# Loading each expert weight unit with one transfer of 16 KB rows in place of two of 8 KB rows

## The chip, the cores and the metric

The kernel runs on one core of one Trainium2 chip. The metric is the device time of one execution in microseconds (us), median over several runs; lower is better. All arithmetic is in float32.

## What is computed

The reference is a small encoder trunk of two layers on 256 tokens of width 1024. Layer 0 is a dilated sliding-window attention followed by a dense SwiGLU; layer 1 is a bidirectional RWKV-7 time mixer followed by a mixture of eight SwiGLU experts, of which each token uses two. Only the last part is touched by the change:

```python
def swiglu(h, w13, w2):
    gate, up = jnp.split(h @ w13, 2, axis=-1)
    return (jax.nn.silu(gate) * up) @ w2

def moe_swiglu(h, router, w13, w2):          # 8 experts, TOP_K = 2, D = 1024, D_FF_EXPERT = 3584
    t = h.reshape(B * S, D)
    logits = (t @ router).astype(jnp.float32)
    top_val, top_idx = lax.top_k(logits, TOP_K)
    gate = jax.nn.softmax(top_val, axis=-1)
    combine = jnp.einsum('tk,tke->te', gate, jax.nn.one_hot(top_idx, N_EXPERTS, dtype=jnp.float32))
    out = jnp.zeros_like(t)
    for e in range(N_EXPERTS):
        out = out + combine[:, e:e + 1] * swiglu(t, w13[e], w2[e])
```

An expert's weights are 1024 x 7168 and 3584 x 1024 floats, 44 MB; all eight are 352 MB, and each is read once.

## The kernel before

All weights pass through a ring of slots in SBUF. A slot holds one **unit**: 128 partitions x 4096 floats (`SLOT`), that is 16 KB per partition and 2 MB in all. SyncE (SP in the profile) issues every weight load from one instruction stream, written out by hand; TensorE (PE) waits for a unit with `arrived(pe, u)` (L566), which waits on the slot's semaphore `slot_full`, multiplies, and counts a semaphore by which SP knows that the slot is free. The first layers use 45 units (`U_DENSE`), loaded by `square` and `ff_unit` in rows of 1 to 4 KB. The experts use 21 units each (`U_EXPERT`), 168 in all, over nine slots taken in turn.

The unit of an expert is either "up" (14 of them: 256 gate and 256 up columns for all 1024 input features) or "down" (7 of them: 512 of the hidden rows for all 1024 outputs). The host has laid out `mw13` and `mw2` so that a unit is one contiguous block of 2 MB in HBM, [128 partitions, 4096 floats]. `expert_plan` (L148) gives the order: ups, with a down after every second one from the fourth up on.

`halves` (L623) issues two transfers, each adding 16 to the slot's semaphore when it has landed, so a slot that has been filled n times stands at 32 n. `tiled_unit` (L705) calls it for an expert's unit with the left and the right half of every row: two transfers of 1 MB, 128 rows of 8 KB each. Both have the same line, L623, in the profile, as have all other weight loads. The loop over the experts' units (L792 to L806) waits, before each unit, until its slot is free (`first_free` for the first nine, `free[before_it[u]]` after that); after the unit with `at == 10` it waits for the gathered tokens and for the previous tokens' buffer, and loads `xe`, the next expert's rows (L806).

Experts stand in a fixed order of room: heavy ones with room for 96 tokens and light ones for 64 alternate, beginning with a heavy and ending with a light one. In `expert` (L1584) a heavy expert's unit is multiplied for tokens 0 to 63 (L1616 for ups, L1591 for downs) and then for 64 to 95 (L1624, L1598); a light one's only for the first 64. The tokens reach `xg` in HBM by four indirect transfers of GpSimd (POOL, L3144) before the first `xe` load; results go to `yd` in HBM (L2073) and come back by four indirect gathers (L3150) during the last expert. After the last unit PE adds the last expert's rows and the residual (L1660, L1664), ACT copies them and stores the output.

A loop for tokens that find no room (`OVER`, L1668) loads its units through `tiled_unit` too; its waits count in `landed`. On these inputs it is passed through without a turn.

The wait count of a unit is `(earlier[u] + 1) * 32`, with `earlier[u]` the number of units that had the slot before.

Of the kernel before, what the change touches and what calls it, by code (L numbers as in the profile page):

```python
# [52 lines left out]
SLOT = 4096  # L53
# [106 lines left out]
def build(nc, x_in, xp_in, pos_in, const_in, mask_in, vec_in, rows_in, qk_rows, qk_cols, wqkv, awo, wrkv, w0, w1, w2, a0, a1, a2,  # L160
          g1, g2, bwo, fw13, fw2, router, mw13, mw2, out):
    ctx = ExitStack()
    with ctx:
# [3 lines left out]
        def sem(name):  # L167
            return ctx.enter_context(nc.semaphore(name))
# [42 lines left out]
        v = m.take(T, GROUPS, 512)  # L211
# [154 lines left out]
        for d in range(2):  # L366
            o = {}
# [42 lines left out]
        slot_full = [sem(f"slot_full{i}") for i in range(R + 3)]  # L410
# [140 lines left out]
        MOE0 = U_DENSE  # L551
# [4 lines left out]
        slot_in_turn = [u % RQ_SLOTS if u < U_QKV else u % R for u in range(MOE0)]  # L556
# [4 lines left out]
            slot_in_turn.append(in_line[0])  # L561
            in_line.rotate(-1)
        slot_in_turn += [v % R for v in range(U_EXPERT)]
        earlier = [slot_in_turn[:u].count(r) for u, r in enumerate(slot_in_turn)]
        before_it = [max((v for v in range(u) if slot_in_turn[v] == r), default=None) for u, r in enumerate(slot_in_turn)]

        def arrived(eng, u):

            eng.wait_ge(slot_full[slot_of(u)], (earlier[u] + 1) * 32)

        def slot_of(u):

            return slot_in_turn[u]

        def unit(u):
            return ring[slot_of(u)]
# [26 lines left out]
        over_uses = [slot_in_turn[MOE_END:].count(r) for r in range(R)]  # L603
# [15 lines left out]
        def _(sp):  # L619
            def halves(u, dst, src):  # L620

                for a, b in zip(dst, src):
                    sp.dma_start(a, b).then_inc(slot_full[slot_of(u)], 16)  # L623
# [31 lines left out]
            for u in range(U_QKV):  # L655
# [9 lines left out]
                if u == 0:  # L665
                    s, w = unit(u).rearrange("p (k n) -> p k n", n=512), wqkv[:, col:col + 512].rearrange("(k p) n -> p k n", p=P)
# [33 lines left out]
            def expert_unit(u, e):  # L700

                kind, g, _ = plans[(u - MOE0) // U_EXPERT][(u - MOE0) % U_EXPERT]
                tiled_unit(u, (mw13 if kind == "up" else mw2)[bass.ds(e, 1), g])

            def tiled_unit(u, w):  # L705

                w, half = w.rearrange("o p n -> p (o n)"), SLOT // 2
                halves(u, (unit(u)[:, 0:half], unit(u)[:, half:]), (w[:, 0:half], w[:, half:]))


            xd = nc.dram_tensor("xd", (16, 8, BLK, BLK), F32).ap()
# [81 lines left out]
            for u in range(MOE0, MOE_END):  # L793
                n, at = (u - MOE0) // U_EXPERT, (u - MOE0) % U_EXPERT
# [36 lines left out]
        def _(pe):  # L831
# [72 lines left out]
            def ff_first_unit(between):  # L904

                arrived(pe, FF0)
                w = unit(FF0).rearrange("p (k n) -> p k n", n=512)
                for t in range(T):
                    for k in range(KB):
                        pe.wait_ge(rms_h, H_DONE[0] + t * KB + max(k + 1, 2))  # L910
                        last = mm(ps[:, 2 * t, :], hT[:, k, t * P:(t + 1) * P], w[:, k, :], start=(k == 0), stop=(k == KB - 1))  # L911
                    last.then_inc(proj_ready, 1)
                    if t == 0:
                        between()

            def ff_first_product(i):

                arrived(pe, FF0 + i)
                if i == 2:
                    pe.wait_ge(hid_sb, 1)  # L920
                elif i > 2:
                    pe.wait_ge(sg_sb, 2 * (i - 2) + 2)
                two_rows_of_blocks(i % 2, tokens_of(0, 0), quarter(FF0 + i, 0, 0), True, False).then_inc(proj_ready, 1)
# [45 lines left out]
            def ff_down():  # L969

                for j in range(FF_DOWNS - 2):
                    arrived(pe, DN0 + j)
                    pe.wait_ge(turned_in, 2 * j + 2)
                    for name in ("P1", "P2", "P6", "P7", "P5", "P3", "P4"):
                        if j == 0 and name == "P1":
                            pe.wait_ge(sg_sb, 2 * FF_UPS - 2)
                        if j == 0 and name == "P2":
                            pe.wait_ge(turned_in, FF_UPS - 1)
                        if j == 0 and name == "P6":
                            ff_turn(FF_UPS - 1)  # L980
                            pe.wait_ge(combined, ff_combination(FF_UPS - 2, "C21"))
                        if j == 0 and name == "P5":
                            pe.wait_ge(combined, ff_combination(FF_UPS - 1, "C11"))
                        if j == 0 and name == "P3":
                            pe.wait_ge(sg_sb, 2 * FF_UPS)
                        if j == 0 and name == "P4":
                            pe.wait_ge(combined, ff_combination(FF_UPS - 1, "C21"))
                        last = down_product(j, name)
                    last.then_inc(dn_ps, 1)
                pair = (FF_DOWNS - 2, FF_DOWNS - 1)  # L990
                for j in pair:
                    arrived(pe, DN0 + j)
                pe.wait_ge(turned_in, FF_UPS)
                for name in ("P1", "P6", "P2", "P5", "P3", "P7", "P4"):
                    for j in pair:
                        last = down_product(j, name)
                    last.then_inc(dn_ps, 1)
# [184 lines left out]
            for k in range(KB):  # L1182
                pe.wait_ge(mix_ready, k + 1)
                for n in range(2):
                    w = unit(RKV0 + n).rearrange("p (k n) -> p k n", n=512)
# [5 lines left out]
            for bank in range(2):  # L1191
                pe.wait_ge(mix_ready, (2 * bank + 3) * KB)
                for k in range(KB):
                    for a, r in enumerate(COLS):
                        j = 2 * bank + a
# [326 lines left out]
            w = [unit(BWO0 + n).rearrange("p (k n) -> p k n", n=512) for n in range(2)]  # L1522
# [38 lines left out]
            def pick_transposes(c, b, chosen):  # L1561

                pe.wait_ge(pick_ok, chosen * 2)
                for t in range(T):
                    last = pe.transpose(ps[:, 4, t * P:(t + 1) * P], pick[:, b, t, :], ident)
                last.then_inc(pickT_ps, 1)

            def gather_half(b, half, width, back=None):
                if half and back is not None:
                    pe.wait_ge(pickT_sb, back)  # L1570
                for k in range(4):
                    f = (4 * half + k) * P
                    last = run(ps[:, (7, 4)[half], k * P:k * P + width], [(xn[:, t, f:f + P], pick[:, b, t, 0:width]) for t in range(T)])
                last.then_inc(picked_ps, 1)

            def scatter(results, b, back, width):

                pe.wait_ge(y_sb, results)
                pe.wait_ge(pickT_sb, back)
                for k in range(4):  # L1580
                    t, h = k // 2, k % 2
                    run(ps[:, (4, 7, 0, 1)[k], :], [(pickT[0:width, b, t, :], yb[0:width, h * 512:(h + 1) * 512])]).then_inc(back_ps, 1)

            def expert(n, runs, results, light, c, b, plan, landed, before_last=None):  # L1584

                per = 2 if light else 3
# [16 lines left out]
                for kind, g, u in plan:  # L1603
                    if kind == "down" and g == GE // 2 - 1 and before_last:
                        before_last()
                    landed(u)
                    if kind == "up":
                        w = unit(u).rearrange("p (k n) -> p k n", n=512)
# [59 lines left out]
            with pe.Fori(0, OVER) as j:  # L1668
                with pe.If(j < many):
                    def landed(u):  # L1670
                        pe.wait_ge(slot_full[slot_of(u)], j * (32 * over_uses[slot_of(u)]) + 32 * (earlier[u] + 1))

                    n = j + EXPERTS
                    pe.wait_ge(back_sb, j * 4 + 4)
                    pick_transposes(n + 1, 0, j + 3)
                    gather_half(0, 0, CAP)
                    gather_half(0, 1, CAP, j + 2)
                    expert(n, j * UPS + RUNS0[FULL], j * 2 + RESULTS0[FULL], False, n + 1, 0, over_plan, landed)
                    scatter(j * 2 + (RESULTS0[FULL] + 2), 0, j + 2, CAP)
# [1511 lines left out]
```

## Time and profile before

| | us |
|---|---|
| median of 3 runs | 1802.97 |
| lowest and highest | 1799.80, 1805.57 |
| the profiled execution, whole | 1802.29 |
| its span, first to last instruction | 1800.6 |
| PE busy in the span | 1650.3 (92%) |
| DVE, ACT, POOL busy | 873.5, 339.2, 236.2 |
| moved by DMA | 471.86 MB |

The span of 1800.6 us and 1.7 us around it make the profiled 1802.29 us, 0.7 us under the median of the runs. In the profile a stretch is given from the span's start. "DMA share" is the mean busy share of the core's 16 DMA engines, as the sum of their packets' times; it can pass 1 where a packet starts before the one ahead of it has ended. A packet is one row of a transfer on one DMA engine; every transfer also writes one small packet per engine, with which it counts its semaphore. The wait table names who waited, at which line, and what released it; SPq is SP's own queue of transfers.

### The profile page before, as it was taken

The numbers are of one execution on the slowest core, as the hardware profiler recorded it, in microseconds if no ns is written. First come the engines' busy times: TensorE is split into PE (matmuls) and PEld (weight loads), VectorE is DVE, ScalarE is ACT, GpSimd is POOL, SyncE is SP. The second block draws the span as 40 slices with busy tenths as digits, with TensorE's granted clock in tenths as the row PEclk, the third lists the DMA queues.
The fourth block names the chain that finished last, engine by engine and source line by source line (L and its number), as shares of the span: only waits on it lengthen the run. The fifth ranks groups of instructions, "written<-read, shape, count | busy, mean of one in ns | idle before, by whom it ended". The sixth has DMA issues, their size and how long they took to land.

```text
span 1800.6 us, 31353 instructions
## 1 busy us (share of the span) xinstructions
PE 1650.3 (92%) x12986; PEld 1082.1 (60%) x12986; DVE 873.5 (49%) x2082; ACT 339.2 (19%) x719; POOL 236.2 (13%) x319
## 2 busy tenths in 40 slices
PE   8999999999999998998999997999779996799877
PEld 6888886788445577877765553554335543355433
DVE  6667653555565476775354435343233533234331
ACT  3334332121011343542210000100000000000001
POOL 2432420100001434453010000000000000000000
PEclk9999999999999999999989999999999999999999
DMA  9452426754640000102759999999999999999995
GB/s 328 176 187 80 155 97 204 234 179 170 180 182 24 24 22 13 31 17 79 285 198 387 419 398 420 419 400 419 394 421 409 403 420 389 421 401 413 419 421 244
DMA packets 137586, 471.86 MB, mean 262 GB/s; under 512 B 30168, under 2 KB 59120, under 8 KB 94432
## 3 DMA queue, kind: packets, MB, share of 16 engines
q1 hardware_dynamic: 133776, 459.32, 66.1%
q0 software_dynamic: 1952, 6.85, 1.2%
q10 hardware_dynamic: 1712, 3.64, 0.5%
q8 instruction: 105, 1.72, 0.4%
q14 instruction: 41, 0.34, 0.1%
HBM read 460.59 MB, written 9.18 MB: 261 GB/s over the span
## 4 chain that ended last, share of the span: by engine, by line
PE 56%; SPq 28%; DMA 7%; DVE 5%; ACT 2%; issue 2%; POOL 0%; DVEq 0%
SPq L623 27%; PE ps L837 12%; PE ps L1019 11%; PE ps L891 10%; DMA arena<-mw 6%; PE ps L1616 6%; PE ps L1624 3%; PE ps L1591 3%; PE ps L1187 2%; PE ps L883 1%; PE ps L1598 1%; PE ps L1548 1%; PE ps L1534 1%; PE ps L1033 1%; PE ps L911 1%
## 5 line engine op out<-in xcount | busy, mean ns | idle before, releaser
L1616 PE MATMUL ps<-arena 128*64 128x256 f32 x3584 | 405.2, 382 | 64.2 <-DMA arena<-mw 64.2
L1616 PEld LDWEIGHTS ps<-arena 128*64 128x64 f32 x3584 | 252.4, 137 | 230.7 <-DMA arena<-mw 95.5
L837 PE MATMUL ps<-arena 128*128 128x128 f32 (+9 forms) x1946 | 276.9, 318 | 19.1 <-DVE arena L2542 9.1
L2884 DVE TENSOR_TENSOR arena<-arena,ps 64x256 f32<-64x256 f32 x140 | 59.5, 426 | 473.5 <-ACT arena L2061 473.4
L837 PEld LDWEIGHTS ps<-arena 128*128 128x128 f32 (+3 forms) x1946 | 219.6, 185 | 72.1 <-issue 39.3
L1591 PE MATMUL ps<-arena 128*64 128x512 f32 x896 | 207.0, 606 | 38.7 <-DMA arena<-mw 38.7
L1019 PE MATMUL ps<-arena 128*128 128x256 f32 x952 | 210.7, 379 | 0.1
L1019 PEld LDWEIGHTS ps<-arena 128*128 128x128 f32 x952 | 178.5, 190 | 23.8 <-issue 0.5
L891 PE MATMUL ps<-arena 128*128 128x256 f32 (+1 forms) x714 | 189.0, 425 | 0.0
L2061 ACT ACTIVATE arena<-ps 64x256 f32<-64x256 f32 x140 | 52.8, 377 | 723.0 <-PE ps L1616 631.0
L891 PEld LDWEIGHTS ps<-arena 128*128 128x128 f32 x714 | 134.8, 190 | 50.6 <-issue 34.4
L1591 PEld LDWEIGHTS ps<-arena 128*64 128x64 f32 x896 | 60.6, 138 | 162.4 <-issue 110.8
L2862 DVE STREAM_TRANSPOSE arena<-arena 32x128 f32<-32x128 f32 x448 | 136.3, 304 | 7.3
L1624 PE MATMUL ps<-arena 128*32 128x256 f32 x1792 | 102.5, 380 | 0.0
L3150 POOL DMA_INDIRECT arena<-yd,arena x4 | 3.8, 953 | 749.6 <-DMA yd<-arena 748.7
L2306 DVE TENSOR_TENSOR arena<-arena 128x1024 f32<-128x1024 f32 (+3 forms) x92 | 86.0, 959 | 22.0 <-PE ps L891 20.9
L1624 PEld LDWEIGHTS ps<-arena 128*32 128x32 f32 x1792 | 55.0, 110 | 44.8 <-issue 10.8
L2873 DVE STREAM_TRANSPOSE arena<-arena 32x64 f32<-32x64 f32 x224 | 53.3, 238 | 3.6
L1598 PE MATMUL ps<-arena 128*32 128x256 f32 x896 | 53.6, 379 | 0.0
L1960 ACT ACTIVATE arena<-ps 128x512 f32<-128x512 f32 (+1 forms) x80 | 43.9, 561 | 44.7 <-PE ps L837 37.1
L2842 DVE STREAM_TRANSPOSE arena<-arena 32x128 f32<-32x128 f32 x136 | 41.2, 303 | 5.1 <-DMA arena<-xg 3.0
L1598 PEld LDWEIGHTS ps<-arena 128*32 128x32 f32 x896 | 28.4, 110 | 22.1 <-issue 3.2
(318 smaller groups left out, 1439.2 us busy)
## 6 DMA issues: line engine op xcount, KB each, us to landing
arena<-mw SPq DMA_DIRECT2D x336, 1024.0 KB, 26.9
arena<-wqkv SPq DMA_DIRECT2D x35, 1024.0 KB, 7.3
arena<-fw SPq DMA_DIRECT2D x32, 1024.0 KB, 7.5
arena<-wrkv SPq DMA_DIRECT2D x12, 1024.0 KB, 7.4
arena<-awo SPq DMA_DIRECT2D x4, 1024.0 KB, 6.4
arena<-bwo SPq DMA_DIRECT2D x4, 1024.0 KB, 9.5
xg<-arena POOLq DMA_DIRECT2D x4, 384.0 KB, 8.5
arena<-rows SPq DMA_DIRECT2D x4, 384.0 KB, 4.7
```

The source lines that it names most:

```text
L623: sp.dma_start(a, b).then_inc(slot_full[slot_of(u)], 16)
L837: last = mm(o, a, b, start=(n == 0), stop=(n == len(pairs) - 1))
L891: last = mm(ps[:, bank, 0:b.shape[2]], a[:, k, :], b[:, k, :], start=(start and k == 0), stop=(stop and k == n - 1), skip_group_check=True)
L1019: last = mm(ps[:, bank, 0:256], a[:, k, :], b[:, k, :], start=(start and k == 0), stop=(stop and k == 3), skip_group_check=True)
L1591: last = mm(ps[r, 5, :], hidT[:, g % 2, k, 0:64], w[:, k, a * 512:(a + 1) * 512], start=(first and k == 0), stop=(end and k == 3), skip_gr ...
L1598: last = mm(ps[r, 6, 0:256], hidT[:, g % 2, k, 64:CAP], w[:, k, a * 256:(a + 1) * 256], start=(first and k == 0), stop=(end and k == 3), s ...
L1616: last = mm(ps[r, g % 4, 0:256], picked[:, b, k, 0:64], w[:, k, a * 256:(a + 1) * 256], start=(k == 0), stop=(k == KB - 1))
L1624: last = mm(ps[r, (7, 4)[p % 2], 0:256], picked[:, b, k, 64:CAP], pair[a % 2][:, k, a // 2 * 256:a // 2 * 256 + 256], start=(k == 0), stop ...
L2306: dve.tensor_tensor(out, a, b, op).then_inc(sums_ok, 1)
L2862: last = dve.transpose(o[:, :, :, 32 * i:32 * i + 32], src[:, :, :, j, :])
L2873: last = dve.transpose(o[:, a, :, 64:CAP], src[:, :, j, :])
L2884: dve.tensor_tensor(hid_e[RH:P, p % 2, i, :], sg_e[RH:P, j % 2, :], ps[RH:P, bank, 0:256], ALU.mult).then_inc(hide_sb, 1)
```

## The change

An expert's unit is loaded by one transfer of [128, 4096 floats] instead of two of [128, 2048]. It adds 16 to the slot's semaphore, not 32, so the counts to wait for become a sum over the slot's earlier units: 32 for each unit of the first layers, 16 for each of an expert (`filled`).

```diff
-        earlier = [slot_in_turn[:u].count(r) for u, r in enumerate(slot_in_turn)]
+        filled = [sum(32 if v < MOE0 else 16 for v in range(u + 1) if slot_in_turn[v] == r) for u, r in enumerate(slot_in_turn)]
...
         def arrived(eng, u):
 
-            eng.wait_ge(slot_full[slot_of(u)], (earlier[u] + 1) * 32)
+            eng.wait_ge(slot_full[slot_of(u)], filled[u])
...
             def tiled_unit(u, w):
 
-                w, half = w.rearrange("o p n -> p (o n)"), SLOT // 2
-                halves(u, (unit(u)[:, 0:half], unit(u)[:, half:]), (w[:, 0:half], w[:, half:]))
+                sp.dma_start(unit(u), w.rearrange("o p n -> p (o n)")).then_inc(slot_full[slot_of(u)], 16)
...
                     def landed(u):
-                        pe.wait_ge(slot_full[slot_of(u)], j * (32 * over_uses[slot_of(u)]) + 32 * (earlier[u] + 1))
+                        pe.wait_ge(slot_full[slot_of(u)], j * (16 * over_uses[slot_of(u)]) + filled[u])
```

## Rows read from the trace of the kernel before

**Rows 1.** The page: span in 40 slices, PE busy tenths, DMA tenths and GB/s

```profile
PE   8999999999999998998999997999779996799877
...
DMA  9452426754640000102759999999999999999995
GB/s 328 176 187 80 155 97 204 234 179 170 180 182 24 24 22 13 31 17 79 285 198 387 419 398 420 419 400 419 394 421 409 403 420 389 421 401 413 419 421 244
```

**Rows 2.** Stretches: us, busy (x count) of PE, PEld, DVE, ACT, POOL, PEclk, DMA share, GB/s

```profile
957.50:960.00 2.50, 2.50 (x26) 1.63 (x24) 0.00 (x0) 0.18 (x1) 0.00 (x0) 1.00 0.20 41
960.00:1080.00 120.00, 120.00 (x1212) 65.40 (x1210) 49.75 (x161) 9.68 (x25) 0.00 (x0) 1.00 1.01 410
1080.00:1160.00 80.00, 65.29 (x582) 33.84 (x580) 36.40 (x136) 5.71 (x14) 0.00 (x0) 1.00 1.01 420
1160.00:1250.00 90.00, 89.77 (x978) 48.20 (x976) 36.69 (x121) 7.60 (x19) 0.00 (x0) 1.00 1.01 410
1250.00:1350.00 100.00, 72.42 (x508) 34.98 (x506) 30.14 (x93) 5.71 (x14) 0.00 (x0) 0.98 1.01 408
1680.00:1784.00 104.00, 78.74 (x580) 39.77 (x578) 30.25 (x80) 6.85 (x17) 3.81 (x4) 0.97 0.97 400
```

**Rows 3.** Waits of PE from 1080 to 1784 (960 to 1080 has none): total, times, longest

```profile
PE ps L1616 <- DMA arena<-mw: 64.2, 47, 2.7
PE ps L1591 <- DMA arena<-mw: 37.7, 24, 3.5
```

**Rows 4.** PE's timeline at the end: start, us, instructions [idle before <- releaser]

```profile
1779.28 3.65 PE L1591 MATMUL ps<-arena 128*64 128x512 f32 x16 [1.25 <-DMA arena<-mw]
...
1784.28 3.65 PE L1591 MATMUL ps<-arena 128*64 128x512 f32 x16 [0.98 <-DMA arena<-mw]
```

**Rows 5.** SP's transfers in order of time, around the experts' start

```profile
848.14 94.31 SPq L623 DMA_DIRECT2D arena<-mw  x22
958.32 0.45 SPq L806 DMA_DIRECT2D arena<-xg  x1
```

**Rows 6.** Waits of SP's queue from 940 to 962

```profile
SPq L806 <- DMA xg<-arena: 15.8, 1, 15.8
```

**Rows 7.** Waits of SP's queue from 960 to 1784

```profile
SPq L623 <- PE ps L1624: 48.6, 8, 9.7
SPq L623 <- PE ps L1591: 18.2, 7, 3.5
```

**Rows 8.** Transfers that touch mw, 1080 to 1784: issue to landing

```profile
DMA to landing us min/median/max: 23.0/27.3/33.1
```

**Rows 9.** DMA from 1300 to 1350 us: 8 KB rows, steady

```profile
DMA packets 2882, 21.01 MB, mean 420 GB/s; under 512 B 320, under 2 KB 320, under 8 KB 320
...
q1 hardware_dynamic: 2879, 20.96, 100.9%
```

**Rows 10.** DMA from 12 to 32 us: 2 KB rows, steady

```profile
DMA packets 3908, 7.77 MB, mean 388 GB/s; under 512 B 118, under 2 KB 118, under 8 KB 3907
...
q1 hardware_dynamic: 3907, 7.76, 105.0%
```

**Rows 11.** Short bursts: 8 KB rows, then 2 KB rows (columns as in rows 2)

```profile
885.00:892.50 7.50, 7.50 (x22) 3.60 (x21) 4.68 (x10) 0.60 (x1) 2.67 (x2) 1.00 1.02 431
507.50:511.00 3.50, 3.50 (x10) 1.52 (x9) 2.56 (x8) 0.43 (x1) 0.00 (x0) 1.00 1.05 405
```

**Rows 12.** DMA from 1281 to 1294 us, one xe load among the units

```profile
DMA packets 638, 4.22 MB, mean 325 GB/s; under 512 B 75, under 2 KB 75, under 8 KB 171
```

**Rows 13.** DMA queues from 700 to 840 us: packets, MB, share

```profile
DMA packets 10891, 2.77 MB, mean 20 GB/s; under 512 B 8948, under 2 KB 10872, under 8 KB 10872
...
q8 instruction: 14, 0.23, 0.7%
```

**Rows 14.** DMA from 410 to 413 us: 4 KB rows

```profile
DMA packets 323, 1.26 MB, mean 419 GB/s; under 512 B 16, under 2 KB 16, under 8 KB 323
```

## The prediction

> **What bounds the kernel now.** I read the 40 slices first. PE is busy 92% of the span and looks like the bound, but from slice 22 on its digits drop to 7 and 6 while the DMA digits stay at 9 and the rate stands at some 400 to 421 GB/s to the end [rows 1]. So the question has to be asked stage by stage. Before the experts the change touches nothing: only the 168 expert units are loaded by the edited function.
>
> Inside the expert stage the stretches show two kinds of time [rows 2]. While a heavy expert is computed (960 to 1080, 1160 to 1250) PE is busy without a gap; while a light one is (1080 to 1160, 1250 to 1350, and the last, 1680 to 1784) PE is busy only 72 to 82%. The DMA share is 1.01 in all of these but the last, whose end has no loads left. The waits agree: PE idles 64.2 + 37.7 = 101.9 us for the units, all of it after 1080 [rows 3], and it does so before the very last ones too, 1.25 and 0.98 us each [rows 4]. A light unit takes PE 3.65 us of matmuls; the unit spacing there is 5.0 us (1779.28 to 1784.28), which is the transfer's pace. Since DMA never stops in a heavy expert and PE catches up in every light one, the end of the stage is set by the DMA chain: first packet after 960, last unit landed at 1784.
>
> Where that chain begins matters. At 957.5 to 960 the rate is 41 GB/s [rows 2]: the queue had run dry, because SP stood 15.8 us at L806 for the token scatter [rows 6]. By then it had issued 22 transfers, 11 units [rows 5]. So 168 - 11 = **157 units** are behind that point, and only their pace shifts the end. After that SP waits for slots (48.6 and 18.2 us [rows 7]), but a transfer lands 27.3 us after its issue [rows 8], some 5.5 units of 5.0 us deep, so SP's waits lie beside a full queue.
>
> **What a packet costs.** This is the whole change: a unit is 128 rows of 16 KB, 8 packets on each of 16 engines, instead of 256 rows of 8 KB, 16 packets on each. The bytes are the same. I take the cost of a packet from two steady stretches with the queue full. With 8 KB rows: 2879 - 320 = 2559 data packets in 50 us on 16 engines, 800 / 2559 = 312.6 ns each [rows 9]. With 2 KB rows: 3907 - 118 = 3789 in 20 us, 320 / 3789 = 84.5 ns each [rows 10]. The same 8 KB as four packets take 338.0 ns, 25.4 ns more for three more packets: **8.5 ns per packet** beside 304.1 ns per 8 KB of bytes. Both figures carry their small semaphore packet per MB, so that it cancels.
>
> A 16 KB packet is then 2 x 304.1 + 8.5 = 616.7 ns against 625.2 now. Per unit 8 packets fewer, 68 ns. One of the two semaphore packets per engine goes as well; the trace has no steady stretch of them alone, so I bound it between 0 (hidden in the overlap that a share of 1.01 shows) and a packet's 8.5 ns, and take 8.5 because the engines have no idle time to hide it in. Sum: 157 x (68 + 8.5) ns = **12.0 us**. Against the profiled 1802.3 us that gives 1790.3, and 0.7 us more against the median: 1791.0.
>
> The bounds of the packet's price. Above: two packets that shared all of the excess, with the semaphore ones not cancelling, would hardly give over 10 ns, 14 us in all. Between: two bursts, where the queue had just filled, run at 431 GB/s with 8 KB rows and 405 with 2 KB [rows 11], that is 8192 x 16 / 431 = 304.1 ns and 80.9 ns, so (4 x 80.9 - 304.1) / 3 = 6.5 ns per packet, 8.2 us for the edit without the semaphore. Below: 0, if the steady pace is not made of packets. The steady stretch is nearest to what the expert stage is, so I take 8.5.
>
> The row also speaks against a rule. A page of the Trainium skill, DMA: Bandwidth & Descriptors (Specifications), has line rate from 512 B up; by it rows of 8 and 16 KB would run alike and the sum would be 0. The same page (Why small descriptors are slow) puts a fixed 3 cycles of an 850 MHz clock on a packet, 3.5 ns; by that estimate the sum is 157 x 8 x 3.5 ns = 4.4 us. The trace agrees with a fixed cost (2 KB rows run at 388 GB/s, not at 420 [rows 9, 10]) but shows it larger.
>
> **The other parts, with what covers them.** The first 11 units load beside PE's own work before and in the first expert, and their end does not set 958: the scatter does. It shares the engines with two units. With larger weight packets the scatter's share of time may fall, so that it ends later than the weights, but the work in front of the 958 point is the same. Cost 0; bounds -1 us and +2.5 us, the latter for 16 of an engine's 4 KB scatter packets left over alone at 3 x 16 / (323 - 16) = 156 ns each [rows 14].
>
> SP issues 157 transfers fewer behind that point. I cost this at nothing: it is ahead of the engines by 27 us of queue [rows 8]. If the queue's depth is counted in packets it will now be deeper in bytes, until the nine slots limit it; the SP waits then move from the queue to L623 waits for PE, with no packet later. SP's wait at L806 for the previous tokens has only the next units queued behind it, and PE would have to lag nine slots for it to bite.
>
> PE: a unit becomes whole when its last packet lands, in both forms, since PE waited for 32 before. No first half was used early. PE's cover is large: 12 us out of its 101.9 us of waits [rows 3], every light unit still waits about 1.2 us less 0.08. The gathers of results at 1692 to 1696 stand beside longer weight packets and may land some 10 us later; their rows are added by DVE from 1721 on. Cost 0.
>
> **Rivals.**
>
> *The pace is set by bytes, not packets* (0.19 with the next one). At the same 8 KB rows the burst runs at 431 and the steady stretch at 420 [rows 9, 11]; something other than the packet costs 2.6% there, and if it is what ends last, a packet's shorter overhead is only waited out. The time is 1801 to 1803. Against it: the steady 2 KB rows are slower again by just the packet's excess. *The edit does not do what it says*: a 16 KB row is cut again into packets of 8 KB; only the semaphore packet goes, 157 x 8.5 ns = 1.3 us, 1801.7.
>
> *The smaller price per packet* (0.17): 6.5 ns from the bursts, or less. 1794.8 by the bursts, which is still a gain beyond the bound; at 4 us it is not, and I give that part 0.05. The page's 3.5 ns would give 1798.6 in the same way.
>
> *Slower: the token loads disturb longer* (0.10). Six times in the stage, when an `xe` load stands among the units, the rate drops to 325 GB/s for 13 us with the engines still busy [rows 12]: 13 x (1 - 325/420) = 2.9 us lost each. Fewer packets run and the share stays, so packets wait for one another. If the length of that stretch goes with the length of the unit's packets, doubling them doubles it: +2.9 x 6 = 17.6 us, against 12.0 gained, 1808.6. It decides from 2.0 us more per load on. For it: nothing but the mechanism; against: the load's own bytes stay the same. *Slower: a 16 KB packet is bad in itself* (0.04). The only packets of that size in the trace, instruction fetches, take 0.7% x 16 x 140 us / 14 = 1.12 us each on quiet engines [rows 13], not 0.62. They are no weight loads, so they are far from this case. If weights did the same, 157 units would cost 157 x 8 x 0.50 = 622 us more; slower begins where a 16 KB packet passes 634 ns.
>
> **How the numbers follow.** A measurement of this kernel tells some 0.3%, 5.4 us, from no change. Forecast 0.50; smaller price 0.17, of which 0.12 count as faster; bytes or a cut row 0.19; slower 0.14. So faster 0.62, same 0.24, slower 0.14. The predicted time is the forecast's, 1791. The low end takes the highest packet price (2 us more) and 3 us of run spread: 1786. The high end passes the no-change case and its spread, 1806, and leaves out the slower ones.
>
> **What the profile after should show.** Some 21,500 data packets fewer; transfers of 2048 KB, 168 of them. In a steady light stretch 425 to 427 GB/s instead of 420, with the DMA share nearer 1.00, and unit spacing at the tail of 4.92 us. PE's waits for mw 12 us less in total; landing times over 27 us if the queue is counted in packets. The queue's dry point stays at 957 to 960. I am wrong if the steady rate stays at 420 (the bytes bind), if packet counts stay (the row was cut), if the 325 GB/s stretches grow, or if the DMA share falls under 1 in the stage, which would mean that SP or a slot became late.

## The result and the profile after

| | before | changed |
|---|---|---|
| median, us | 1802.58 (5 runs) | 1792.98 (5 runs) |
| lowest, us | 1799.80 | 1790.88 |
| profiled execution, whole / span, us | 1802.29 / 1800.6 | 1792.25 / 1790.4 |

The forecast was 1791.0 us, in a range of 1786 to 1806; the median is 1792.98. The ratio of the times is 0.9936, with a 95% interval of 0.9922 to 0.9950: faster by 0.5 to 0.8%. (One execution of the changed kernel ran at a granted clock of 0.56, took 2849.6 us and is left out of the ratio.)

The page of the changed kernel, as in [rows 1], and its list of transfers:

```profile
PE   8999999999999998988999998999679997799867
...
DMA  8542516854650110100768999999999999999995
GB/s 305 202 163 78 182 62 221 246 174 156 205 181 25 26 26 10 34 17 13 271 248 351 425 406 426 426 407 427 400 427 425 402 427 399 426 411 413 426 426 243
DMA packets 113390, 471.82 MB, mean 264 GB/s; under 512 B 27480, under 2 KB 56432, under 8 KB 91744
...
arena<-mw SPq DMA_DIRECT2D x168, 2048.0 KB, 36.4
```

The plateau that stood at 419 to 421 GB/s stands at 425 to 427. Before there were 137,586 packets; 24,196 are gone, 21,504 of them (168 x 128) data packets and 2,688 (168 x 16) semaphore packets. So the 16 KB row was not cut into packets of 8 KB, and there is one transfer of 2048 KB per unit, 168 in all.

SP's transfers around the experts' start, then PE's last steps, against [rows 5] and [rows 4]:

```profile
852.41 95.70 SPq L707 DMA_DIRECT2D arena<-mw  x11
960.79 0.45 SPq L805 DMA_DIRECT2D arena<-xg  x1
```

```profile
1769.87 3.65 PE L1590 MATMUL ps<-arena 128*64 128x512 f32 x16 [1.19 <-DMA arena<-mw]
1773.45 0.44 PE L1564 MATMUL ps<-arena 128*128 128x128 f32 x2
1774.78 3.65 PE L1590 MATMUL ps<-arena 128*64 128x512 f32 x16 [0.89 <-DMA arena<-mw]
```

I call **the stage** what lies from the issue of the first `xe` load to the first matmul of the last unit. In these two executions the queue is dry at that issue (DMA share 0.20 from 957.5 to 960 before, 0.54 from 960 to 962.5 now), so that they can be compared: 1784.28 - 958.32 = 826.0 us before, 1774.78 - 960.79 = 814.0 us now, 12.0 us less. It began 2.5 us later, because the layer before ended later in this execution: the first expert unit was issued at 852.4, not 848.1. Nothing is changed ahead of it, and the same start moves in other runs too (852.9 in `halves_xe128`, whose code up to there is that of the kernel before). And the work after it took 15.6 in place of 16.3 us. So the span: -12.0 + 2.5 - 0.7 = -10.2 us.

Waits of PE from 960 us on, to set against [rows 3]:

```profile
PE ps L1615 <- DMA arena<-mw: 59.6, 41, 3.9
PE ps L1590 <- DMA arena<-mw: 29.2, 24, 2.7
```

They sum to 88.8 us, 13.1 less than before: PE waits less by about what the units gained.

### The profile page after: what moved, and what is told of

Same layout as the page of the kernel before. It is cut to its first block, busy times and chain, and to the rows that moved or that the text cites. A ratio compares the mean times of both kernels' runs of the same rounds, so it can differ in the third digit from the quotient of the medians.

```text
span 1790.4 us, 30891 instructions
## 1 busy us (share of the span) xinstructions
PE 1651.7 (92%) x12986; PEld 1084.5 (61%) x12986; DVE 872.3 (49%) x2082; ACT 338.7 (19%) x719; POOL 235.4 (13%) x319
## 4 chain that ended last, share of the span: by engine, by line
PE 65%; DMA 27%; DVE 5%; ACT 2%; issue 1%; SPq 0%; POOL 0%; DVEq 0%
DMA arena<-mw 26%; PE ps L836 12%; PE ps L1018 11%; PE ps L890 10%; PE ps L1615 10%; PE ps L1590 5%; PE ps L1623 4%; PE ps L1186 2%; PE ps L1597 2%; PE ps L882 1%; PE ps L1032 1%; PE ps L1533 1%; PE ps L1547 1%; PE ps L910 1%; PE ps L844 1%
## 5 line engine op out<-in xcount | busy, mean ns | idle before, releaser
L1623 PEld LDWEIGHTS ps<-arena 128*32 128x32 f32 x1792 | 55.0, 110 | 44.8 <-issue 10.8
L3012 POOL TENSOR_TENSOR arena<-arena 128x128 f32<-128x128 f32 x24 | 20.7, 864 | 161.2 <-DVE arena L2209 161.2
```

What stands on the lines that cost most here:

```text
L1623: last = mm(ps[r, (7, 4)[p % 2], 0:256], picked[:, b, k, 64:CAP], pair[a % 2][:, k, a // 2 * 256:a // 2 * 256 + 256], start=(k == 0), stop ...
```

## The experiments

All start from the changed kernel unless said. The quiet stretch from 1210 to 1240 us, with no `xe` load and no result store in it, serves as the gauge of pace in all of them. Kernel before, then changed:

```profile
DMA packets 1727, 12.59 MB, mean 420 GB/s; under 512 B 193, under 2 KB 193, under 8 KB 193
```

```profile
DMA packets 883, 12.80 MB, mean 427 GB/s; under 512 B 102, under 2 KB 102, under 8 KB 102
```

### Packet size alone

**One transfer, 8 KB packets.** The host lays a unit out as two blocks of [128, 2048], so that one transfer must fetch each partition's row in two pieces:

```diff
-                sp.dma_start(unit(u), w.rearrange("o p n -> p (o n)")).then_inc(slot_full[slot_of(u)], 16)
+                sp.dma_start(unit(u).rearrange("p (h n) -> p h n", h=2), w.rearrange("o h p n -> p (o h) n")).then_inc(slot_full[slot_of(u)], 16)
...
-        "mw13": a["m_w13"][0].reshape(EXPERTS, KB, P, 2, GE, 256).transpose(0, 4, 2, 1, 3, 5).reshape(EXPERTS, GE, P, SLOT),
+        "mw13": a["m_w13"][0].reshape(EXPERTS, KB, P, 2, GE, 256).transpose(0, 4, 2, 1, 3, 5).reshape(EXPERTS, GE, P, 2, SLOT // 2).transpose(0, 1, 3, 2, 4),
```

(`mw2` likewise.)

> One transfer per expert unit as in the changed kernel, but each row arrives as two packets of 8 KB. Measured so far, from the issue of the first xe load to the first matmul of the last unit: 826.0 us before (two transfers, 8 KB packets), 814.0 us changed (one transfer, 16 KB packets). Theory A (each data packet costs 8.5 ns on its engine, whatever transfer it is in): 8 packets more per unit than in the changed kernel, 157 x 8 x 8.5 ns = 10.7 us, so a stage of 824.7 us and about 1801.3 us, a steady rate of 420 to 421 GB/s. Theory B (the gain came from half as many transfers: fewer issues, fewer semaphore packets, a queue deeper in bytes): a stage of about 814 us and about 1793 us.

Measured: median 1802.58 us, ratio to the kernel before 0.9992 (95% interval 0.9977 to 1.0006; so in all that follows). The gain is gone although there is one transfer per unit. The quiet stretch:

```profile
DMA packets 1628, 12.59 MB, mean 420 GB/s; under 512 B 94, under 2 KB 94, under 8 KB 94
```

The semaphore packets are halved (94 against 193) and the bytes are the same 12.59 MB as before. Theory B falls. The profiled stage was 828.3 us, some 4 us over the expectation and 2 over the kernel before at the same pace. Here the queue was not dry when the first `xe` load was issued at 955.67: the DMA share was 1.02 from 955 to 957.5, so this stage still holds the end of the first 11 units. The same is so for `one4k` (issue at 952.80, share 1.05 from 955 to 957.5) and `four4k`. A stage that begins with a full queue comes out some us too long.

**4 KB and 2 KB packets** (`h=4` and `h=8` in the same edit).

> One transfer per expert unit, each row as four packets of 4 KB. Theory A: 24 packets more per unit than in the changed kernel, 157 x 24 x 8.5 ns = 32.0 us, so a stage of 846 us (814.0 changed), about 1825 us, and a steady rate of about 408 GB/s. Theory B (number of transfers decides): about 814 us and 1793 us. Theory C (pace set by bytes from 4 KB rows up, as the short burst of 4 KB rows at 419 GB/s could suggest): no slower than 8 KB rows, stage 826 us.

> One transfer per expert unit, each row as eight packets of 2 KB. From 4, 8 and 16 KB packets the quiet rates were 408.5, 419.8 and 426.4 GB/s, 641.7, 624.5 and 614.8 ns for 16 KB on one engine: 8.6 ns for each packet from 4 to 8 KB, 9.7 ns from 8 to 16 KB. A fixed cost of 8.5 to 9 ns gives 641.7 + 4 x 8.6 = 676 ns, 388 GB/s, and 157 x 8 x 61 ns = 77 us over the changed kernel, about 1870 us. If small packets get worse than in proportion, more.

Measured: with 4 KB packets 1828.37 us, ratio 1.0141 (1.0115 to 1.0168), stage 851.8 us; with 2 KB packets one execution of 1869.0 us, stage 895.1 us. The quiet stretch with 4 KB, then with 2 KB packets:

```profile
DMA packets 3079, 12.26 MB, mean 409 GB/s; under 512 B 93, under 2 KB 93, under 8 KB 3077
```

```profile
DMA packets 5715, 11.57 MB, mean 386 GB/s; under 512 B 87, under 2 KB 87, under 8 KB 5712
```

Sixteen engines move 16 x 16,384 B = 0.2621 MB while each moves one 16 KB row, so a row takes 30 x 0.2621 / MB microseconds. Thirty microseconds are short for this: other kernels with the same 16 KB packets move 12.76 to 12.80 MB in them, a spread of 1.9 ns per row. So the table also has the sum over all stretches of 25 us or more between the `xe` loads, without 2.5 us at each end (small result stores included):

| packets per 16 KB row | MB in 30 us | ns per row | MB in all quiet stretches | ns per row | for each packet more |
|---|---|---|---|---|---|
| 1 (changed) | 12.80 | 614.4 | 283.65 in 665.0 us | 614.6 | |
| 2 (one8k) | 12.59 | 624.6 | 294.11 in 700.0 us | 623.9 | 9.3 |
| 4 (one4k) | 12.26 | 641.5 | 291.07 in 712.5 us | 641.7 | 8.9 |
| 8 (one2k) | 11.57 | 679.7 | 286.18 in 740.0 us | 677.9 | 9.0 |

A straight line: from one to eight packets 63.3 ns for seven more, 9.0 ns each. From 2 to 16 KB the pace is bytes plus a fixed price per packet. For 2 KB packets it gives 814.0 + 157 x 8 x 63.3 ns = 893.5 us of stage, where 895.1 was measured. The kernel before, with two semaphore packets per unit where one8k has one, takes 624.2 ns (297.12 MB in 707.5 us), 9.6 ns more than the changed one.

Two kernels from further below have long quiet stretches and show the same step, 614.7 ns and 624.1 ns: 765 us with 16 KB packets (`no_xe`, 970 to 1735), then 550 us with 8 KB packets (`halves_xe128`, 1045 to 1595):

```profile
DMA packets 23359, 326.27 MB, mean 426 GB/s; under 512 B 2623, under 2 KB 2623, under 8 KB 3711
```

```profile
DMA packets 32342, 231.04 MB, mean 420 GB/s; under 512 B 3616, under 2 KB 3616, under 8 KB 4736
```

**Four transfers of 4 KB rows** (the unit cut into quarters of each row, 64 counts per slot and unit):

```diff
-                sp.dma_start(unit(u), w.rearrange("o p n -> p (o n)")).then_inc(slot_full[slot_of(u)], 16)
+                w = w.rearrange("o p n -> p (o n)")
+                for k in range(0, SLOT, SLOT // 4):
+                    sp.dma_start(unit(u)[:, k:k + SLOT // 4], w[:, k:k + SLOT // 4]).then_inc(slot_full[slot_of(u)], 16)
```

> Four transfers per expert unit, each 128 rows of 4 KB: the same data packets as one4k, with three semaphore packets more per unit and engine. The prediction took a semaphore packet at 8.5 ns: 157 x 3 x 8.5 ns = 4.0 us over one4k. If semaphore packets hide under the overlap of packets: the same as one4k. Beyond that, if the queue's depth is counted in packets, landing times near 27 us x 1/2 per transfer's share of bytes, and no change of pace.

Measured: 1827.38 us, ratio 1.0134 (1.0108 to 1.0159), the same as one transfer of 4 KB packets within the intervals.

```profile
DMA packets 3351, 12.24 MB, mean 408 GB/s; under 512 B 373, under 2 KB 373, under 8 KB 3347
```

373 semaphore packets stand against 93, and the bytes fall by 0.02 of 12.26 MB, which is no more than the 30 us can resolve. Over all quiet stretches a row takes 641.8 ns (293.07 MB in 717.5 us) against 641.7 with one transfer: 8 rows x 0.1 ns for three semaphore packets, 0.3 ns each. The kernel before against one8k gives 8 x 0.3 = 2.4 ns for one. So a semaphore packet costs 3 ns at most, by an estimate from these row times, and not the 8.5 that the prediction took. The two times alone would not tell it: 4.0 us is inside their intervals. The number of transfers, and of SP's issues, is worth next to nothing here.

### The depth of the queue

In the changed kernel SP no longer stands behind a full queue but behind the slots. Its waits in the stage, the first two of four, to set against [rows 7], and the time to landing of the transfers that touch `mw` against [rows 8]:

```profile
SPq L707 <- PE ps L1623: 268.0, 26, 13.1
SPq L707 <- PE ps L1615: 209.6, 52, 8.4
```

```profile
DMA to landing us min/median/max: 7.7/36.4/44.9
```

So the queue is deeper in bytes, 36 us in place of 27, as the packet-counted depth foretold. Does that carry part of the gain? An added wait puts the depth back, with 16 KB packets:

```diff
+                if u >= MOE0 + 11:
+                    sp.wait_ge(slot_full[slot_of(u - 5)], filled[u - 5])
                 expert_unit(u, e)
```

> The changed kernel, with SP waiting before each expert unit (from the twelfth on) until the fifth unit before it has landed, so that at most five units, 25 us of loads, are queued, about the depth of the kernel before; 16 KB packets stay. Theory A (packets alone): the pace is kept, stage 814 us and about 1793 us, landing times fall from 36 us to about 24 us. Theory D (the deeper queue gave part of the gain, by keeping engines busy across skews or xe loads): part of the 12 us comes back, up to a stage of 826 us and 1803 us.

Measured: 1792.44 us, ratio 0.9928 (0.9906 to 0.9950), as the changed kernel. The loads landed 24.3 us after issue in the quiet stretch, and moved at the same pace:

```profile
DMA packets 875, 12.77 MB, mean 426 GB/s; under 512 B 95, under 2 KB 95, under 8 KB 95
arena<-mw SPq DMA_DIRECT2D x6, 2048.0 KB, 24.3
```

The pace in the quiet stretches does not hang on the depth, and the ratio leaves at most some 3 us for it, no large part of the gain. The one profiled execution was the slowest of the six (1799.19 us, stage 818.6 us, 4.6 more than changed). Its loss around the `xe` loads, counted as in the next section, is 20 us against 16.5, some 3 of the 4.6. Whether the shallower queue makes these stretches longer, or this execution was a slow one, is not shown.

### The stretches of low rate

The rival that ended slower stood on the `xe` loads. From 1275 to 1295 us, before and then changed, with both an `xe` load's packets and the units' (compare [rows 12]):

```profile
1275.00:1295.00 20.00, 13.82 (x88) 6.18 (x86) 6.47 (x21) 0.75 (x2) 0.00 (x0) 0.91 1.02 362
```

```profile
1275.00:1295.00 20.00, 11.00 (x80) 5.49 (x80) 7.47 (x23) 0.75 (x2) 0.00 (x0) 0.99 1.01 366
```

They are as low as before and no lower. Over the whole stage, cut into stretches of 2.5 us, those under 95.5% of the quiet rate lose 15.9 us before and 16.8 us changed. The place where the cutting starts moves such a sum by up to 1 us (16.1 to 16.7 and 15.9 to 16.8 with four starts), so this is no difference. The rival's 17.6 us more did not come. But the loss is larger than the change's gain, so I looked for its cause.

**Without the loads** (all but the first left out, so the later experts compute on the second one's rows and the output is not that of the reference; the result stores stay in, though the expectation says that a part of them goes):

```diff
-                    sp.dma_start(xe[0:ROOM[n + 1]], xg[ROWS0[n + 1]:ROWS0[n + 2], :]).then_inc(xe_in, 16)
+                    if n == 0:
+                        sp.dma_start(xe[0:ROOM[n + 1]], xg[ROWS0[n + 1]:ROWS0[n + 2], :]).then_inc(xe_in, 16)
...
-                    dve.wait_ge(xe_in, n * 16 + 16)
+                    dve.wait_ge(xe_in, 16)
```

> The changed kernel with the token rows (xe) loaded for the second expert only; the six later loads and their share of the results are left out, so experts three to eight work on the second one's rows. In the changed kernel the stage loses 16.8 us in the stretches of low rate around the xe loads (12.5 us in whole 2.5 us windows under 95.5% of the quiet rate is the least). Theory X (the xe loads cause these stretches): they vanish but for the first, stage about 814 - 14 - 4 us of the loads' own bytes = 796 to 800 us, about 1777 us. Theory Y (something else that comes once per expert, such as result stores or instruction fetches): the stretches stay, stage 810 us or more, about 1790 us.

Measured: 1772.01 us, ratio 0.9826 (0.9808 to 0.9844); stage 1753.47 - 960.08 = 793.4 us; 0.1 us lost in low stretches. Theory X holds: the loads cost 20.6 us of stage, of which their own 2.0 MB at 426 GB/s are 4.6. The other 16.0 us are the loss counted in the low stretches.

**From another source** (the first 1024 floats of some weight rows in place of the tokens; the output is again not that of the reference):

```diff
-                    sp.dma_start(xe[0:ROOM[n + 1]], xg[ROWS0[n + 1]:ROWS0[n + 2], :]).then_inc(xe_in, 16)
+                    sp.dma_start(xe[0:ROOM[n + 1]], mw2[0, 0, 0:ROOM[n + 1], 0:D]).then_inc(xe_in, 16)
```

> The changed kernel with the xe loads reading the first 1024 floats of 96 or 64 rows of an expert's weights instead of xg, into the same partitions; the experts after the first then work on these numbers. Theory Q (the source xg is slow): the low stretches vanish, stage about 800 us. Theory P (the destination's partitions collide): they stay at some 16 us, stage about 814 us.

Measured: one execution of 1793.18 us, 16.6 us lost, the same stretch as low. It isn't reading `xg`:

```profile
1275.00:1295.00 20.00, 12.69 (x80) 6.24 (x80) 6.89 (x22) 0.75 (x2) 0.00 (x0) 0.91 1.01 366
```

**Over 128 partitions:**

```diff
-                    sp.dma_start(xe[0:ROOM[n + 1]], xg[ROWS0[n + 1]:ROWS0[n + 2], :]).then_inc(xe_in, 16)
+                    many_rows = P if n + 2 < EXPERTS else ROOM[n + 1]
+                    sp.dma_start(xe[0:many_rows], xg[ROWS0[n + 1]:ROWS0[n + 1] + many_rows, :]).then_inc(xe_in, 16)
```

> The changed kernel with every xe load but the last made over all 128 partitions (128 rows of 4 KB, 512 KB) instead of 96 or 64; the rows beyond an expert's room are not used. Theory P (a load over 96 or 64 partitions gives the 16 engines partitions that collide with those of the unit loads): the low stretches vanish for the 128-row loads although more bytes move, stage 814 - 14 + 3 = about 803 us, about 1782 us. Theory Q (reading xg is what is slow): the stretches stay or grow with the bytes, stage 814 to 820 us, 1793 us or more.

Measured: 1781.49 us, ratio to the kernel before 0.9877 (0.9858 to 0.9897), stage 802.6 us, 3.2 us lost. More bytes, and the low stretch is gone:

```profile
1275.00:1295.00 20.00, 15.04 (x106) 7.83 (x102) 7.47 (x23) 0.88 (x3) 0.00 (x0) 0.91 1.00 424
```

**Every unit in two transfers of 64 partitions**, which tells packet size from the partitions once more:

```diff
-                sp.dma_start(unit(u), w.rearrange("o p n -> p (o n)")).then_inc(slot_full[slot_of(u)], 16)
+                w = w.rearrange("o p n -> p (o n)")
+                for r in COLS:
+                    sp.dma_start(unit(u)[r], w[r]).then_inc(slot_full[slot_of(u)], 16)
```

> Two transfers per expert unit as before the change, but cut by partitions: 64 rows of 16 KB each, so the packets stay at 16 KB. Theory A (packets alone decide): as the changed kernel plus one semaphore packet per unit and engine, under 1.3 us: stage 814 to 815 us, about 1794 us. Theory P (a transfer over 64 partitions makes engines collide): much slower, rate of the low stretches, 340 GB/s, everywhere: 157 x 1.25 us = about 200 us more, near 1990 us.

Measured: 2240.43 us, the median of four from 2167.59 to 2441.73, so no interval is given. The quiet stretch:

```profile
DMA packets 502, 6.56 MB, mean 219 GB/s; under 512 B 101, under 2 KB 101, under 8 KB 101
q1 hardware_dynamic: 501, 6.55, 100.5%
```

The engines are busy all the time and move 219 GB/s, half of 427. The slices of the page show the rate climbing later, while the DMA share stays at 1.01 (1500 to 1600, 360 GB/s):

```profile
GB/s 309 178 114 153 116 224 181 175 184 135 20 33 15 26 18 159 214 233 213 227 224 216 220 224 226 248 299 342 374 350 309 328 305 362 350 297 290 248 248 153
```

Theory P holds in its direction and was put too low: 375 us lost in the fastest of the four and 447 by their median, not 200. The packets are the same 16 KB as in the changed kernel; what differs is that each transfer reaches 64 partitions. The Trainium skill (SBUF — State Buffer, Door 1: The DMA port swizzle) says that a transfer's bandwidth goes with how many of 16 ports its partitions reach, and that partitions 0 to 63 reach only half of them. The half rate of 219 in the quiet stretch agrees; the 374 GB/s of a later slice, with the same loads, doesn't, and why the rate climbs stays open. No trace here shows a port, so the port itself is argued. What the runs show is narrower: transfers over 64 partitions alone run at half the rate for hundreds of us, and one over 64 or 96 among those over 128 lowers the rate of all together.

### The best version, and whether the two effects add

**All seven loads over 128 partitions.** The last one would read rows of `xg` that nothing has written; GpSimd sets them to zero with the others:

```diff
+            pool.dma_start(xg[ROWS0[FULL]:ROWS0[FULL] + RH, :].rearrange("p (a n) -> p a n", n=P), zero[0:RH].unsqueeze(1).broadcast_to([RH, KB, P])).then_inc(xg_zero, 16)
...
-            pool.wait_ge(xg_zero, EXPERTS * 16)
+            pool.wait_ge(xg_zero, EXPERTS * 16 + 16)
...
-                    sp.dma_start(xe[0:ROOM[n + 1]], xg[ROWS0[n + 1]:ROWS0[n + 2], :]).then_inc(xe_in, 16)
+                    sp.dma_start(xe, xg[ROWS0[n + 1]:ROWS0[n + 1] + P, :]).then_inc(xe_in, 16)
```

(ACT's wait on `xg_zero` likewise.)

> The changed kernel with all seven xe loads over 128 partitions; the 64 rows of xg behind the last expert's are set to zero with the others, so that the last load too can take 128. With six of seven (xe128) the stage was 1762.88 - 960.26 = 802.6 us and 3.2 us were still lost, most of it at the seventh load, around 1589 to 1602. Theory P: that goes too, 2 to 3 us less: stage 800 us, about 1779 us. If the last stretch had another cause, it stays and the time is that of xe128, 1781.5 us.

Measured: 1779.46 us, ratio 0.9866 (0.9844 to 0.9888), 1.2 us lost in low stretches, stage 1761.87 - 958.98 = 802.9 us. The low stretch at the seventh load went; the gain over 1781.5 is inside both intervals and the stage, where I expected 800, did not get shorter. The two stages begin differently (the DMA share from 957.5 to 960 was 1.03 in `xe128` and 0.82 here), so a us or two between them is not told.

**The kernel before with six loads over 128 partitions:**

> The kernel before (two transfers of 8 KB rows) with six of the seven xe loads over 128 partitions. If the packet's cost and the loss at the xe loads are independent: 1802.6 - 11.5 = about 1791 us, stage 826 - 11.4 = 814.6 us, quiet rate 420 GB/s. If the loss at the xe loads depended on the 16 KB packets, the gain is not 11.5 us here.

Measured: 1791.62 us, ratio 0.9926 (0.9899 to 0.9952). The stage was 1775.25 - 958.92 = 816.3 us, 1.7 over the expectation; it too began with a full queue (share 1.03 from 957.5 to 960). The 8 KB packets keep their old pace:

```profile
DMA packets 1722, 12.58 MB, mean 419 GB/s; under 512 B 189, under 2 KB 189, under 8 KB 189
```

The two effects add up, as far as the intervals tell: the packets are worth 9.6 us by the medians, the wider loads 11.5 us on the changed kernel and 10.0 on the kernel before, both together 22.2.

## Why the prediction was right

- **The bound.** Right. From the dry point on the stage is a chain of units at DMA's pace; it got 12.0 us shorter, and PE waited 13.1 us less. The whole kernel gained 9.6 us by the medians and 10.2 in the profiled executions, where 12.0 was forecast; in the profile the difference is the later start of the stage (2.5 us, not caused by the change) less the 0.7 us gained behind it.
- **157 units count, the first 11 don't.** Right as far as seen. SP still stood at the `xe` load for the scatter, 12.6 us in place of 15.8; the queue ran dry at some 961 us and not at 957 to 960, by the same later start.
- **The packet's price.** Taken as 8.5 ns from 2 KB and 8 KB rows; measured 9.3 ns for the step made here and 9.0 ns over four sizes. 157 x 8 x 9.3 ns = 11.7 us where 10.7 stood.
- **The semaphore packet.** Mis-sized: 8.5 ns taken, because the engines have no idle time to hide it in; at most 3 ns by the row times, so some 0.4 us and not 1.3. The two errors cancel: 10.7 + 1.3 = 12.0 was forecast, and the row times of the kernels before and changed give 157 x 8 x 9.6 ns = 12.1. That the sum met the 12.0 us of the profiled stage to the tenth is luck; that it came within an us is not.
- **The rivals.** Bytes alone are refuted by the straight line down to 2 KB, and with them, for these sizes, the line rate from 512 B up of the Trainium skill (DMA: Bandwidth & Descriptors, Specifications): 2 KB packets ran at 386 GB/s and 16 KB packets at 427. The 3.5 ns estimated from the same page of the Trainium skill (Why small descriptors are slow) are too small, 9.0 measured. The cut row is refuted by 21,504 fewer data packets. The longer `xe` stretches did not come: 16.8 against 15.9 us lost, not doubled. The slow 16 KB packet of the instruction fetches did not come for weights: 614.6 ns, where slower began at 634.
- **Where a stall goes.** SP's waits moved to the slots, and the DMA share stayed at 1, so they cost nothing. The gathers of results landed later, 19.3 us after issue by the median against 12.2, and DVE now stands 5.0 us for them, which PE doesn't feel:

```profile
DVE arena L2948 <- DMA arena<-yd,arena: 5.0, 1, 5.0
```

## What to carry to other kernels

Where the DMA share stands at 1 for a long stage, take the price of a packet from two stretches with different row lengths and multiply by the packets that an edit removes; here the estimate met the measured stage within 1 us in 800 and the time within 2 in 1800. Take the prices from long stretches: the difference looked for is 1.5% of the rate. With the queue full, it was the row length that counted and not the number of transfers. Then look at small loads in the same queue: a load over 64 or 96 partitions of 0.3 MB cost as much as 1.5 MB of units, and filling it up to 128 partitions with rows that nobody reads was worth as much as the whole change.

## What the runs showed of the hardware that was not expected

- A packet costs 9.0 ns beside its bytes, the same from 2 to 16 KB, and a semaphore packet 3 ns at most.
- The burst of 8 KB rows at 431 GB/s for 7.5 us [rows 11] stays unexplained: bytes plus 9.0 ns a packet give 420, as all long stretches of 8 KB rows do.
- Two transfers over 64 partitions each, in place of one over 128, halve the rate in the quiet stretch, 219 against 427 GB/s, with the queue's packets at 100.5% of the engines' time. A DMA share of 1 shows engines with packets under way, and not that they move what they can.
- Six `xe` loads of 64 or 96 partitions lost 16 us beyond their bytes, from either of two sources, and 1 to 3 us when filled up to 128.
- Before the last unit the engines do not end together. With no load left to issue, the share falls to about a half some 10 us before the last unit's first matmul, in both kernels. Changed, from 1762.5 us on:

```profile
1762.50:1765.00 2.50, 1.31 (x15) 0.57 (x9) 0.43 (x1) 0.38 (x1) 0.00 (x0) 1.00 0.74 315
1765.00:1767.50 2.50, 2.50 (x24) 1.72 (x26) 0.00 (x0) 0.00 (x0) 0.00 (x0) 1.00 0.57 242
1767.50:1770.00 2.50, 1.31 (x14) 0.64 (x12) 0.82 (x3) 0.38 (x1) 0.00 (x0) 1.00 0.59 249
```
